# Sliding, differential and top-k attention in one kernel: key scalings ahead of selection rounds, value evictions ahead of other work

## The reference

```
q, k, v = split(h @ w_in)                      # layer 0: differential attention, 8 pairs of heads
q = rope(rms_norm(q)) / 8;  k = rope(rms_norm(k))
p = softmax(where(mask, q @ k.T, -inf))        # mask: by chunks of 64 tokens
o = (p[head 0] - lam * p[head 1]) @ v          # per pair
x = x + (rms_norm(o) * gain) @ w_out           # norm over the 128 columns of a pair
x = x + relu(rms_norm(x) @ w1)**2 @ w2

score = sum_h w_idx[h] * relu(q_idx[h] @ k_idx.T)   # layer 1: each query keeps its 128 best keys
keep = top_k(where(mask, score, -inf), 128)
o = softmax(q @ k[keep].T) @ v[keep]           # 16 heads
x = x + o @ w_out;  x = x + relu(rms_norm(x) @ w1)**2 @ w2
```

## Time and profile before

| what | value |
|---|---|
| median of 3 runs | 2325.9 us (2325.01 to 2327.94) |
| the profiled execution | 2326.93 us |
| its span, first to last instruction | 2325.2 us |
| instructions | 28626 |
| mean granted TensorE clock | 0.993 |
| PE / DVE / ACT busy | 97% / 53% / 33% |

### The profile page before, as it was taken

How to read it: one execution, slowest core, us unless ns; L and a number is a source line. 1 busy time by engine, 2 the same in 40 slices (tenths; PEclk the granted TensorE clock), 3 DMA queues, 4 the chain that set the end, 5 groups by cost and what they waited for, 6 DMA issues and landing times.

```text
span 2325.2 us, 28626 instructions
## 1 busy us (share of the span) xinstructions
PE 2265.9 (97%) x11717; PEld 1838.3 (79%) x11717; DVE 1242.8 (53%) x1504; ACT 776.8 (33%) x1013; POOL 152.6 (7%) x109
## 2 busy tenths in 40 slices
PE   7999999989999999999988999999999999999999
PEld 6888888867788888887875788888876868888888
DVE  5434446587544346475567554444568764544443
ACT  4212234335322332343237321222334573222222
POOL 2000001030100100020000100000100301000000
PEclk9999999999999999999999999999999999999999
DMA  5232322320223222233320132232233201323322
GB/s 166 90 105 94 98 74 92 104 73 11 82 91 107 92 90 90 90 100 100 95 87 1 55 109 90 93 106 90 78 113 77 69 19 55 109 90 96 103 90 73
DMA packets 193443, 200.58 MB, mean 86 GB/s; under 512 B 6274, under 2 KB 188640, under 8 KB 193346
## 3 DMA queue, kind: packets, MB, share of 16 engines
q1 hardware_dynamic: 193346, 199.22, 27.3%
HBM read 191.93 MB, written 2.10 MB: 83 GB/s over the span
## 4 chain that ended last, share of the span: by engine, by line
PE 89%; DVE 7%; ACT 2%; issue 1%; DMA 1%; SPq 0%; POOL 0%; DVEq 0%; ACTq 0%
PE psum L622 87%; DVE sm L2335 1%; DVE w_lo L263 1%; ACT free_h L1384 1%; DVE free_x L1848 0%; PE psum L1109 0%; ACT w_hi L255 0%; DVE free_h L1851 0%; DVE arena L1848 0%; DVE free_x L2440 0%; DMA w_raw<-in_ffn_w_gate 0%; DVE rstd L1866 0%; DVE sm L2438 0%; DMA arena<-in_x 0%; DVE sm L2176 0%
## 5 line engine op out<-in xcount | busy, mean ns | idle before, releaser
L622 PE MATMUL psum<-xg_lo,w_hi 128*128 128x512 f32 x1552 | 602.2, 391 | 0.4 <-ACT free_x L1384 0.4
L622 PE MATMUL psum<-xg_hi,w_hi 128*128 128x512 f32 x1504 | 590.7, 393 | 6.2 <-DVE w_lo L263 2.8
L622 PE MATMUL psum<-xg_hi,w_lo 128*128 128x512 f32 x1504 | 586.7, 390 | 0.0
L255 ACT ACTIVATE w_hi<-w_raw 128x2048 fp32r<-128x2048 f32 (+1 forms) x181 | 344.4, 1903 | 501.5 <-PE psum L622 492.8
L263 DVE TENSOR_TENSOR w_lo<-w_raw,w_hi 128x2048 fp32r<-128x2048 f32 (+1 forms) x179 | 411.5, 2299 | 169.5 <-ACT w_hi L255 166.3
L622 PE MATMUL psum<-h_hi,w_hi 128*128 128x512 f32 x1144 | 451.8, 395 | 0.3 <-DVE h_lo L1848 0.3
L622 PE MATMUL psum<-h_hi,w_lo 128*128 128x512 f32 x1144 | 445.7, 390 | 0.0
L622 PE MATMUL psum<-h_lo,w_hi 128*128 128x512 f32 x1144 | 445.5, 389 | 0.0
L622 PEld LDWEIGHTS psum<-xg_lo,w_hi 128*128 128x128 f32 x1552 | 292.1, 188 | 62.6 <-ACT free_x L1384 1.4
L622 PEld LDWEIGHTS psum<-xg_hi,w_hi 128*128 128x128 f32 x1504 | 283.2, 188 | 71.0 <-issue 6.5
L622 PEld LDWEIGHTS psum<-xg_hi,w_lo 128*128 128x128 f32 x1504 | 283.1, 188 | 59.4
(11 more groups left out here) (305 smaller groups left out, 2159.5 us busy)
## 6 DMA issues: line engine op xcount, KB each, us to landing
w_raw<-in_mlp_w SPq DMA_DIRECT2D x64, 1024.0 KB, 5.4
w_raw<-in_ffn_w_gate SPq DMA_DIRECT2D x22, 1024.0 KB, 5.3
w_raw<-in_ffn_w_up SPq DMA_DIRECT2D x22, 1024.0 KB, 5.3
w_raw<-in_ffn_w_down SPq DMA_DIRECT2D x16, 1024.0 KB, 5.1
w_raw<-in_diff_w_in SPq DMA_DIRECT2D x12, 1024.0 KB, 5.2
w_raw<-in_w_in SPq DMA_DIRECT2D x9, 1024.0 KB, 5.2
w_raw<-in_dsa_w_in SPq DMA_DIRECT2D x9, 1024.0 KB, 5.3
w_raw<-in_ffn_w_down SPq DMA_DIRECT2D x8, 768.0 KB, 4.4
```

What stands on the lines that cost most here:

```text
L255: e.activation(w_hi[:, c % 2, 0:n], w_raw[:, c % 2, 0:n], ACT.Copy).then_inc(sem("hi_done"), 1)
L622: return pe.matmul(out, lhsT, rhs, start=start, stop=stop)
```

## The change

Sliding part. SP loads only block 0 of `wout1` ahead of the key swap, and the rest after it. PE no longer waits for the eviction of c + 9 ahead of the eight units but ahead of the scores of unit 3. DVE makes `a1_norm(0)` and `a1_norm(1)` ahead of that eviction; the split of block c + 11 (second of `wout1`) goes behind the level sums on DVE and behind the last level's exponentials on ACT.

Differential part. The first unit's scores are issued after token tile 2 of the last value block. DVE and ACT each evict two of the four token tiles of that block. The rope of the last key half is cut into its two steps. The split of block c + 13 (second of `wout2`) is made in four parts inside the loop. The norm "sub" becomes two norms of four tiles, "sua" and "sub": sua's statistics go to a free corner of `bank[5]` at unit 20, ACT loads the table of the root at unit 30, and for both norms ACT copies the high rows of `rs_hi` while DVE copies the low ones. Blocks 0 and 1 of `wout2` are interleaved: k-tiles 0 to 3 of both, then 4 to 7. The split of block 2 of `wout2` goes ahead of the next norm's work.

Top-k part. The rounds of row 1 are no longer all made ahead of the first key scaling but spread between scalings and ropes; three rounds of row 2 go from there to after `first_lo(0)`, and one round of row 3 goes from before to after the eviction of the value half.

The core of the diff (left out: the semaphore bookkeeping of "sua" and of the parts, `stat_rows`, and the first unit's own buffer for its probabilities):

```diff
@@ SP
-            plain("wout1", io["w_out"][0], 2)
+            plain("wout1", io["w_out"][0], 1)
...
-            plain("wout1", io["w_out"][0], 4, first=2)
+            plain("wout1", io["w_out"][0], 4, first=1)
@@ PE
-            pe.wait_ge(sem("evac"), c + 10)
+            pe.wait_ge(sem("evac"), c + 9)
...
             for u in range(8):
+                if u == 1:
+                    pe.wait_ge(sem("evac"), c + 10)
...
+                    if not dsa and u == 20:
+                        gn_stat("sua", 0)
+                        gn_stat("sua", 1)
...
+            def first_pair(t):
+                if t == 2:
+                    pe.wait_ge(sem("evac"), c + 11)
+                    pairs_attention("a2", False, early=True)
+
+            tok_blk(c + 11, mid=lambda t: rope_turn(3) if t == 3 else None, a=xg(4), after=first_pair)
             pe.wait_ge(sem("evac"), c + 12)
+            pe.wait_ge(sem("v_half"), 1)
...
-            for i in range(4):
-                gn_stat("sub", i)
-            for i in range(3):
-                gn_step("sub", i)
-            blk(at["wout2"], ...)
-            wout("wout2", 5, {}, first=1)
+            gn_stat("sub", 0)
+            pe.wait_ge(*use("a2", "_oc", 7))
+            gn_step("sua", 0)
+            gn_stat("sub", 1)
+            gn_step("sua", 1)
+            gn_step("sua", 2)
+            begin(at["wout2"])
+            for k in range(4):
+                pe.wait_ge(*use("sua", "_out", k + 1))
+                wout2_half(0, (k,))
+                if k == 0:
+                    gn_step("sua", 3)
+            begin(at["wout2"] + 1)
+            wout2_half(1, (0, 1))
+            gn_step("sub", 0)
+            wout2_half(1, (2,))
+            gn_step("sub", 1)
+            wout2_half(1, (3,))
+            gn_step("sub", 2)
+            for k in range(4, KT):
+                pe.wait_ge(*use("sub", "_out", k - 3))
+                last = wout2_half(0, (k,))
+                if k == 4:
+                    gn_step("sub", 3)
+            last.then_inc(sem("pe_blk"), 1)
+            wout2_half(1, range(4, KT)).then_inc(sem("pe_blk"), 1)
+            wout("wout2", 5, {}, first=2)
@@ ACT
+            def gn_spread_hi(name):
+                act.wait_ge(sem("rs_rounded"), SHARED.index(name) + 1)
+                for n in range(NT):
+                    last = a(rs_hi[0:16, n * P:(n + 1) * P], rs_part[32 * n:32 * n + 16, 0, :], ACT.Copy)
+                last.then_inc(sem("rs_shared"), 1)
...
             gla_exp(6, 10)
+            hi(act, c + 11)
...
-                    if name == "wout1" and i == 0:
+                    if name in ("wout1", "wout2") and i == 0:
                         hi(act, c + 2)
...
                 exp(0)
+                    v_last()
...
+                    if not dsa and u in (1, 3, 5, 7):
+                        hi_part(act, at["diff"] + 13, u // 2)
+                    if not dsa and u == 30:
+                        sqrt_table()
                 if not dsa:
-                    sqrt_table()
+                    gn_rms("sua")
@@ DVE
-            for i in range(2):
-                evac_scaled(c + 8 + i, gog[:, 2 * i:2 * i + 2, :])
-                lo(dve, c + 10 + i)
-                if i == 0:
-                    gla_keys(5)
-                    a1_max(0)
-                    a1_max(1)
+            evac_scaled(c + 8, gog[:, 0:2, :])
+            lo(dve, c + 10)
+            gla_keys(5)
+            a1_max(0)
+            a1_max(1)
+            a1_norm(0)
+            a1_norm(1)
+            evac_scaled(c + 9, gog[:, 2:4, :])
...
             for l in USED[3:]:
                 gla_acc(l)
+            lo(dve, c + 11)
...
-            pairs_attention("a2", False)
+            pairs_attention("a2", False, early=True)
+            rope_sin(3)
+            v_last()
+            pairs_attention("a2", False, between=lambda u: lo_part(dve, c + 13, u // 2 - 1) if u in (3, 5, 7, 9) else None)
+            gn_split("sua", h2_hi, h2_lo)
             gn_split("sub", h2_hi, h2_lo)
...
             gn_rsqrt("sk")
-            take(1, 16)
-            mask(1)
             gn_scale("sk", 0)
             gn_scale("sk", 1)
+            take(1, 2)
             lo(dve, c + 9)
             rope(PACK["sq"])
             gn_scale("sk", 2)
             gn_scale("sk", 3)
+            take(1, 1)
             rope(PACK["sq"] + 1)
             gn_scale("sk", 4)
             gn_scale("sk", 5)
-            take(2, 1)
+            take(1, 1)
             gn_scale("sk", 6)
             gn_scale("sk", 7)
-            take(2, 1)
+            take(1, 1)
             rope(PACK["sk"])
-            take(2, 1)
+            take(1, 16)
+            mask(1)
             rope(PACK["sk"] + 1)
...
             pairs_attention("a3", True, early=True)
-            take(3, 2)
+            take(3, 1)
             dve.wait_ge(sem("pe_blk"), c + 12)
...
             last.then_inc(sem("v_half3"), 1)
-            take(3, 2)
+            take(3, 3)
```

More of the change, by code:

```diff
@@ L1153, in pairs_attention @@
                     return
-                if not dsa:
-                    scores(0)
                 scores(1)
@@ L1451, in gn_square @@
                 src = GN[name]["pairs"][i]
-                if name != "sub" and use(name, "_msq", i)[1]:
+                if name not in ("sua", "sub") and use(name, "_msq", i)[1]:
                     act.wait_ge(*use(name, "_msq", i))
@@ L1515, in _ @@
             stats(1)
-            for i in range(10):
+            for i in range(9):
                 hi(act, c + 2 + i)
@@ L1592, in wout @@
                     fin(p, 2 * i + 1)
-                    if name != "wout1" or i:
+                    if name not in ("wout1", "wout2") or i:
                         hi(act, c + 2 + i)
@@ L1640, in _ @@
             stats(4)
-            for i in range(12):
+            for i in range(11):
                 hi(act, c + 2 + i)
@@ L1647, in _, with v_last @@
                     gn_rms("dk" if i == 7 else "dq")
+            def v_last():
+                act.wait_ge(sem("pe_blk"), c + 12)
+                for t in (2, 3):
+                    last = a(v2[:, t, 3 * BC:4 * BC], two(c + 11, 1)[:, (t % 2) * BC:(t % 2 + 1) * BC], ACT.Copy,
+                             scale=rstd_tok[:, t:t + 1])
+                last.then_inc(sem("v_half"), 1)
             def pairs_attention(name, dsa):
@@ L1658, in exp @@
                         g, n = units[u]
-                        row = probs3(u, cc, n) if dsa else free_x2[:, 2 * (u % 3) + cc, 0:w]
-                        last = a(row, bank[2 * ((u + dsa) % 2) + cc][:, 0:w], ACT.Exp,
+                        row = probs3(u, cc, n) if dsa else free_h2[:, 8 + cc, 0:w] if u == 0 else free_x2[:, 2 * (u % 3) + cc, 0:w]
+                        last = a(row, bank[2 * ((u + 1) % 2) + cc][:, 0:w], ACT.Exp,
                                  scale=rs_q[:, n, 2 * g + cc:2 * g + cc + 1] if dsa else 1.0,
@@ L1893, in residual @@
                 last.then_inc(sem("evac"), 1)
-                split_first = c + i == at["wout1"]
+                split_first = c + i in (at["wout1"], at["wout2"])
                 if split_first:
@@ L2319, in _, with v_last @@
             gn_rsqrt("dk")
-            for i in range(4):
+            for i in range(3):
                 evac_tok(c + 8 + i, v2, i * BC)
                 lo(dve, c + 10 + i)
-                for t in (range(4), range(4, 8), (), ())[i]:
+                for t in (range(4), range(4, 8), ())[i]:
                     gn_scale("dk", t)
-                if i in (1, 2):
-                    rope(1 + i)
+                if i == 1:
+                    rope(2)
+            def v_last():
+                dve.wait_ge(sem("pe_blk"), c + 12)
+                for t in (0, 1):
+                    last = ts(v2[:, t, 3 * BC:4 * BC], two(c + 11, 0)[:, t * BC:(t + 1) * BC], rstd_tok[:, t:t + 1], None, ALU.mult)
+                last.then_inc(sem("evac"), 1)
             def pairs_attention(name, dsa, between=None, early=False):
@@ L2375, in pairs_attention @@
                 if not dsa:
-                    smax(0)
+                    norm(0)
+                    rope_add(3)
                 smax(1)
                 for u, (g, n) in enumerate(units):
-                    if not dsa:
+                    if not dsa and u:
                         norm(u)
```

74 lines of the change are left out of this document (54 added, 20 removed).

## The result

| | before | after |
|---|---|---|
| median of 5 runs | 2326.28 us (2325.01 to 2327.94) | 2309.82 us (2308.26 to 2311.06) |
| the profiled execution | 2326.93 us, span 2325.2 | 2308.26 us, span 2306.5 |
| mean granted clock | 0.993 | 0.997 |

The ratio is 0.9929, with a 95% interval from 0.9914 to 0.9943: 16.5 us less by the medians. The forecast was 2307.0, with a range of 2301 to 2314. The two profiled executions lie 18.7 us apart, more than the medians do; an early mark shows why.

A forecast was written before the change was run, and what follows sets the result against it. PE was busy 2265.9 of 2325.2 us, so edits count only where PE waits or runs at its lower clock. Gains of 11.1 + 2.6 + 3.3 + 2.0 = 19.0 gave 2307 us; range 2303 to 2311, with two rivals' sides 2301 to 2314.

The forecast's parts named there:

- Sliding, 11.1: Sliding attention: early key swap and two norms ahead of the eviction start norm 2 earlier on DVE; 11.1 us gained.
- Bounds: Sliding attention: gain between 6.5 us (only the two stalls and the clock) and 16.1 (all idle, both slow stretches).
- rival A: Sliding loop moves with PE, isn't limited by DVE from norm 2: only 6.5 us there, 2311.5 us; chance 0.14.
- 58.65 of 73: Sliding attention: DVE's busy us from 528.94 on, as the forecast put it, working nearly without gaps.
- Moved splits, 0: Split of `wout1` block 1 moved behind the level sums: covered by DVE idle, no cost; uncovered at most 4.2 us.
- Entry, 4.3: Differential attention's entry: earlier scores, shared eviction and split moved away bring the wide maximum at 1208.00 4.3 us earlier.
- Loop, minus 1.7: Differential attention's loop: two uncovered split parts lose 1.2 us, the statistics at unit 20 lose 0.5.
- Rival D: Pair loop: denser waits drop PE to 1.2 GHz, 28 us over eight groups, 2335 us; chance 0.02.
- Exit, 3.3: Differential attention's exit: `wout2` starts at 1279.0, 3.1 us earlier; with interleaved blocks 3.3 taken, bounds 5.9 and 0.
- Top-k, 2.0: Top-k layer: PE saves 4.5 us, DVE gives 2.4, new wait 3.1; 2.0 taken, bounds 4.5 and minus 1.3.
- Rival C: Clock stays up at the exit (2.3 us) and PE keeps its 4.5 us in top-k: 2302 us; chance 0.05.
- B: Work pushed into the loops isn't covered: parts cost 2.4 us, top-k loses 1.3; 2311.5 us, chance 0.14.

The follow-up runs named there:

- s_all: The kernel before with the whole sliding part of the change and nothing else; 2315.56 us, ratio 0.9951.
- The two halves: The kernel before with only the key swap's DMA issued ahead of the second `wout1` load, 2321.87 us; with only the rest of the sliding part, 2320.66 us.
- diff: The kernel before with only the differential part of the change; 2320.72 us, ratio 0.9973.
- warm: The changed kernel with nine unused matmuls of 128x512 added in PE's waits at the entry of the differential attention; 2307.38 us, ratio 0.9919.
- parts: The changed kernel with the `wout2` low split's parts after units 5, 9, 13, 17 and sua's statistics ahead of unit 21's transposes; 2307.51 us, ratio 0.9919.
- topk: The kernel before with only the top-k part of the change; 2324.17 us, ratio 0.9992.
- exitw: The changed kernel with 14 unused matmuls of 128x512 added in PE's waits at the exit of the pair loop; 2304.03 us, ratio 0.9907.
- s_norms: The kernel before with the sliding part's order changes on DVE, PE and ACT only, DMA order unchanged; 2320.66 us, ratio 0.9977.

## Why the prediction was right

*Sliding, 11.1.* It is 11.4, and the mechanism is the one given: DVE's order decides from norm 2 on, and it starts at 515.90 in a trace whose early mark lies 1.6 lower, so 517.5 by the clock of before, against 517.8 forecast. Bounds and rival A are answered by s_all. What the forecast held against A, 58.65 of 73, is DVE's share of the whole stretch with the idle 8.34 in it; from 530 to 546 it is 15.5 of 16, and that bears the argument. The two halves are worth 4.7 and 6.3 alone, which the forecast had not told apart. The 1.3 lost again at the entry is in no term.

*Moved splits, 0.* Right: there is no wait for `w_lo` at `wout1`.

*Entry, 4.3.* The order and the starts hold where the clock does: diff and warm give 4.1. In the kernel after it was 2.5. The step that failed is that the clock was not part of this term: I had PE's work there at the durations of the full clock, with two waits of about a us in it, and only gave the clock a price where I saw a single long wait. The 1.6 lost here are the largest error of the sum. That 4.1 and not 2.5 could have come out (diff has the same waits) also says that part of this error is chance.

*Loop, minus 1.7.* Minus 1.25: the parts cost 0.42 and 0.47 in the first two groups (forecast 0.6 each), the statistics 0.37 (0.5). That parts behind n = 1 units are free is shown by parts. Rival D, the loop at 1.2 GHz, didn't come: the clock is 1.00 from 1192 on.

*Exit, 3.3.* 2.8: 3.0 up to the start of `wout2` (forecast 3.1), then minus 0.2 where the forecast had plus 0.2. Whether the interleaving took that is not shown, since this stage varies by 1.0 where nothing is changed and the clock was low in it both times. The table load took 1.28, and ACT's next instruction starts at 1257.93, 0.02 behind its end; the one ahead of it ended 0.02 before it began. The earlier trace rows show only the load; what followed it in the kernel before is this row of ACT:

```profile
1272.60 0.20 ACT L1384 ACTIVATE sm<-eps 128x1 f32<-128x1 f32 x1
```

The Trainium skill's page "ScalarE: Activation LUTs" (section "What ACT_TABLE_LOAD costs") adds a drain to the load; neither trace has one on either side of it.

*Top-k, 2.0.* 1.6, in after and in topk alike. DVE gave 2.4 and 2.9 at the two maxima (forecast 2.4); the new wait is 3.04 (3.1), and the clock fell behind it, as feared. That took 1.2: exitw, where it didn't fall behind the same wait, is that much shorter.

The forecast was 2.8 below the result. The terms forecast 19.0 and the stages give 17.0: entry 1.8 too high, exit and top-k 0.9 together, sliding and loop 0.7 too low. Of the rest, 0.4 is that two more runs put the median of before at 2326.28, and 0.5 is how the executions stand to their medians. Rival C, in which the clock stays up at the exit, didn't happen by itself; exitw shows that it can be had, for 2.1 of the 2.3 it was priced at. B is out: most of what was pushed into the loops was covered.

It stays open why the clock stood at 1.00 behind the wait of 3.04 in exitw and fell behind the same wait in after, and likewise at the entry in diff and after. What makes the first mark differ by 2.8 us between executions stays open too.

## What to carry to other kernels

Where an engine idles for a block (8.34 us of DVE here), list what stands behind that block in its own order and needs nothing of it: that work is free, and it adds to what a faster block brings. A bundle of small work that is moved into a loop should be dealt out one piece per period, behind the unit with slack, before it is called free. And an exit or entry with two or three waits of a us should be priced at both clocks; where the clock stayed up with one wait shortened (0.6 us on DVE) or filled with matmuls that nobody reads, the stage was 1.6 to 3 us shorter.

## What the runs showed of the hardware

The granted clock fell behind short waits: after 0.98 and 1.27, with 0.47 to follow, it was at 1.2 GHz until 1192. But the waits didn't settle it. Three times the same waits had both outcomes: 0.98, 1.27 and 0.47 (a fall in after, 1.00 in diff), 3.04 (a fall in after, 1.00 in exitw), and 2.65 or 2.67 (a fall in before, 1.00 in s_norms). The Trainium skill's page "TensorE: Matmul & The Clock Gate" (section "HAM oscillation — how this bites in real kernels") tells of one long idle stretch in each turn of a loop; that idling brings the slow clock back agrees, but the length of the longest wait was no guide here. Stages without a change in them kept their length to 0.01 us where the clock was up (the loop: 53.60 or 53.61 in five kernels), and varied by up to 2.1 us where it fell at one moment or another (entry: 24.23 to 26.37 in the kernels that leave it as it was). A difference of a us in such a stage says nothing about an edit until the clock's rows have been read. Nine filler matmuls of 512 columns, 1.08 us for the first four and 1.41 for the other five, cost nothing: the entry took 20.14 with them in warm and without them in diff.
